# Two layers of a hybrid trunk on one core: reordered start, reordered down projections, key heads first

## The chip, the cores and the metric

The kernel runs on one core of one Trainium2 chip. The metric is the device time of one execution in microseconds, median of three runs; lower is better.

## The reference

The reference is a decoder trunk of two pre-norm residual layers over one sequence of 512 tokens with 1024 features, all in float32.

- Each layer adds `mixer(RMSNorm(x)) @ w_out` and then `(silu(h @ w_gate) * (h @ w_up)) @ w_down` with `h = RMSNorm(x)` and 2816 hidden features. A final RMSNorm follows.
- Layer 0 (even) mixes a gated 31-tap causal convolution with layer norm and differential attention (4 heads, rotary embedding).
- Layer 1 (odd) mixes a gated delta rule and forgetting attention, 4 heads of 128 each. For the delta rule, queries, keys and values go through a 4-tap causal convolution and SiLU. Queries and keys are then normalised by the root of their own sum of squares over the 128 features of a head, plus 1e-6. Two gates per head and token are computed from 12 extra columns of the input projection: `beta` (a sigmoid) and `g` (minus exp(a_log) times a softplus); forgetting attention has a third, `log_f`. `g` is summed cumulatively inside chunks, `log_f` over the whole sequence.

## The kernel before

**Layout.** Activations lie with features on partitions and tokens in the free dimension: `xT` and its scaled form `HH` are 8 chunks of 128 features by 512 tokens. Every weight and every activation that enters a large product is split into a high part (rounded to fp32r) and a low part (the rest), and a product is three matmuls: high by high, high by low, low by high (`product`, L1484). ScalarE makes the high part of a weight tile (`hi`), VectorE the low part (`lo`).

**Weight stream.** The weights come as 196 tiles of 128 by 1024 (512 KB) in the order in which they are used. SyncE's queue loads them through two raw buffers (the first tiles through two more, `first_raw`); the split copies lie in a ring of four, `wring`. A tile `t` is loaded once the low part of tile `t - 2` is done, and is split once TensorE has used tile `t - 4` (`tile_used`). Counted semaphores tie all of it together.

**Start (L485 to L506 SyncE, L669 on ScalarE, L1053 on VectorE, L1585 on TensorE).** The loads are `vec` (286 columns of per-channel constants, 143 KB), then chunks of x and weight tiles in turn. Three matmuls of 512 columns on zeros run first (`WARM`). Then come the value products of layer 0: four tiles of two chunks each, each chunk multiplied for 4 blocks of 128 tokens into banks 0 to 3 of PSUM, 96 matmuls. Only the first tile is handled in halves. The sum of squares for the norm is collected beside it (`ssq`), summed over features by eight small matmuls (`norm_stats`, at the entry "norm" of `even_order`, L131), and its reciprocal root (`rtok`) is spread over the partitions by `norm_spread`. All engines walk the same written order `even_order()`, each doing its own part of an entry: at ("v", a) ScalarE and VectorE split tile a + 4, at ("cw", c) VectorE builds filter weights.

**Feed-forward.** `gate_up` uses banks 0 to 3 of PSUM in turn, one per tile; VectorE multiplies each by the norm while copying it out (L993, counted by `evacuated`). The down product of layer 0 (`down`, L1728) holds its sums in all eight banks, one for each chunk of output features; that of layer 1 (`token_down`, L1998) also holds eight, two for each block of 128 tokens. Both wait, before their first matmul, for the last of the evacuations of gate and up. In the last four tiles of layer 1 the product goes bank by bank, and the first bank takes each of the four tiles as it arrives.

**Odd layer, first part (TensorE L1787 to L1831, ScalarE L783 to L831, VectorE L1276 to L1310).** Twelve tiles e = 0 to 11 give the convolution inputs: e = 0 to 3 queries, 4 to 7 keys, 8 to 11 values; a thirteenth tile (`HEAD_TILE`, with e = 3) gives the 12 gate columns. For each e, TensorE runs 24 matmuls. VectorE copies the result out (`cin`), splits a weight tile and runs taps 1 to 3 (L1289); ScalarE splits a weight tile, runs tap 0 (L799) and SiLU (L810). For queries and keys ScalarE then squares the result (L815), and TensorE sums the squares over the features by matmuls with one column (`token_sum`, 8 instructions for each e, since a float32 matmul is two). Keys and values are transposed on TensorE (`tok_transpose`, from e = 6 on) and copied back by ScalarE (`tok_copy`, L786). The gate values are computed in four steps on VectorE (`gates_1` to `gates_4`, at e = 5, 6, 7 and 9) with Exp and Ln on ScalarE in between. Their sums over time are matmuls with triangular and all-one matrices at e = 8: 4 instructions for `g`, 20 for `log_f`. `delta_scalars` (VectorE, e = 10) makes the scale factors; the transpose of `pairs` on TensorE (L1830, e = 11) waits for it. After that the delta rule, the attention and the remaining tiles run in an order written out as the string `PLAN`.

Of the kernel before, what the change touches and what calls it, by code (L numbers as in the profile page):

```python
# [19 lines left out]
P = 128  # L20
# [34 lines left out]
WARM = 3  # L55
# [75 lines left out]
def even_order():  # L131

    order = []
    order += [("v", 0), ("cw", 0), ("v", 1), ("cw", 1), ("v", 2), ("norm", 0), ("v", 3), ("norm_bc", 0), ("v_evac", 0), ("cw", 2)]
# [68 lines left out]
PLAN = ("ktttttkatbtatbtttttattattbtbttababttatabttabtatbabatbattabeeooaeotaeebooteeooaeeooeaoabteettootbeeab"  # L203
# [64 lines left out]
def build(nc, x_d, w_d, vec_d, row_d, const_d, rope_d, final_d, out_d):  # L268
# [54 lines left out]
    gtok, q = at("gtok", [NB, H], f32, q)  # L323
    lftok, q = at("lftok", [NB, H], f32, q)
    scal, q = at("scal", [6, NB, H], f32, q)
    total, cum, forget = scal[:, 0], scal[:, 1], scal[:, 2]
    kscal, qeps = (scal[:, 3], scal[:, 5]), scal[:, 4]
    gexp, q = at("gexp", [3, NB, H], f32, q)
    l2s, q = at("l2s", [NB, 8], f32, q)
# [47 lines left out]
    hrow, _ = at("hrow", [S], f32, at_z)  # L377
    rows, q = at("rows", [H, P], f32r, at_A + 3 * 2 * S * 4)
# [74 lines left out]
    x_loaded = [sem(f"x_loaded{n}") for n in range(5)]  # L453
    X_PART = (0, 1, 2, 2, 3, 3, 4, 4)
    first_loaded = [sem(f"first_loaded{n}") for n in range(FIRST - RAW)]
    gdn_mm, gdn_act, gdn_dve, gdn_pool = [[sem(f"gdn{n}_{e}") for n in range(2)] for e in ("products", "act", "dve", "pool")]
    const_loaded, vec_loaded, rope_loaded, small_loaded = map(sem, ("const_loaded", "vec_loaded", "rope_loaded", "small_loaded"))
# [31 lines left out]
    def _(sp):  # L489
# [4 lines left out]
        sp.dma_start(vec[:], vec_d).then_inc(vec_loaded, 16)  # L494
        load_x(0)
        sp.dma_start(raw[:, 0, 0:S], w_d[0][:, 0:S]).then_inc(sem("half_loaded"), 16)
        load_x(1)
        sp.dma_start(raw[:, 0, S:TILE], w_d[0][:, S:TILE]).then_inc(raw_loaded[0], 16)
        load_x(2)
        sp.dma_start(raw[:, 1], w_d[1]).then_inc(raw_loaded[1], 16)  # L500
        load_x(3)
        sp.dma_start(first_raw[:, 0], w_d[2]).then_inc(first_loaded[0], 16)
        load_x(4)
        sp.dma_start(first_raw[:, 1], w_d[3]).then_inc(first_loaded[1], 16)
        sp.dma_start(consts[:, 0:3].rearrange("p a b -> p (a b)"), const_d[:, 0:3 * P]).then_inc(const_loaded, 16)
        sp.dma_start(rowv[0:1, :], row_d).then_inc(small_loaded, 16)  # L506
# [92 lines left out]
    def _(act):  # L599
# [72 lines left out]
        for n in range(KD):  # L672
            act.wait_ge(x_loaded[X_PART[n]], 16)
            feed_hi_(0, n)
            if n < 2:
                act.wait_ge(raw_loaded[0] if n else sem("half_loaded"), 16)
                ins = nc.scalar.activation(wring[:, 0, 0, n * S:(n + 1) * S], raw[:, 0, n * S:(n + 1) * S], ACT.Copy)  # L677
                ins.then_inc(hi_ready[0] if n else sem("first_hi"), 1)
            elif n % 2 == 0:
                hi(n // 2)  # L680
            if n % 2:
                feed_square(0, n - 1)
                feed_square(0, n)
        def diff_exp(u):
# [98 lines left out]
        def tok_copy(m):  # L783

            act.wait_ge(sem("tok_t"), m + 1)
            nc.scalar.activation((ktok, vtok)[m // 4][:, :, m % 4], PS[:, TOK_BANK[m]].rearrange("p (b c) -> p b c", b=NB),  # L786
                                 ACT.Copy).then_inc(sem("tok_ready"), 1)

        for e in range(12):
            if e >= 7:  # L790
                tok_copy(e - 7)
# [10 lines left out]

            h = e % H
            act.wait_ge(sem("gconv_done"), e + 1)
            if e >= 10:
                act.wait_ge(sem("tok_t"), e - 5)
            if e in (8, 9):
                act.wait_ge(sem("l2_mm"), e - 1)
            dst = (qT[:, h], kT[:, h], sqb[:, e % 2])[e // 4]
            nc.scalar.activation(dst, hbuf[:, e % 2], ACT.Silu).then_inc(sem("gsilu"), 1)  # L810
            if e < 8:
                act.wait_ge(sem("gsilu"), e + 1)
                if e >= 2:
                    act.wait_ge(sem("l2_mm"), e - 1)
# [1280 lines left out]
```

## Time and profile before

| | us |
|---|---|
| median of 3 runs (1287.69 to 1289.47) | 1288.94 |
| the profiled execution | 1287.33 |
| its span, first to last instruction | 1285.5 |
| TensorE busy (6195 matmul instructions) | 1268.4 |
| VectorE busy | 671.3 |
| ScalarE busy | 493.6 |
| 16 DMA engines, mean rate | 91 GB/s |

An engine that is busy for nearly the whole span sets the time by the sum of its instructions; what it waits for is then read from the list of its waits, and what it does from a timeline of the stretch. A float32 matmul appears as two instructions, one of fp32r as one.

### The profile page before, as it was taken

The numbers are of one execution on the slowest core, as the hardware profiler recorded it, in microseconds if no ns is written. First come the engines' busy times: TensorE is split into PE (matmuls) and PEld (weight loads), VectorE is DVE, ScalarE is ACT, GpSimd is POOL, SyncE is SP. The second block draws the span as 40 slices with busy tenths as digits, with TensorE's granted clock in tenths as the row PEclk, the third lists the DMA queues.
The fourth block names the chain that finished last, engine by engine and source line by source line (L and its number), as shares of the span: only waits on it lengthen the run. The fifth ranks groups of instructions, "written<-read, shape, count | busy, mean of one in ns | idle before, by whom it ended". The sixth has DMA issues, their size and how long they took to land.

```text
span 1285.5 us, 16497 instructions
## 1 busy us (share of the span) xinstructions
PE 1268.4 (99%) x6195; PEld 1028.6 (80%) x6195; DVE 671.3 (52%) x967; ACT 493.6 (38%) x786; POOL 9.9 (1%) x17
## 2 busy tenths in 40 slices
PE   8999999999999999999999999999999999999998
PEld 6776648888888878888887988888888888887886
DVE  6677786544444442227757657545564444443224
ACT  6353455433333221115455244453433333322113
POOL 0000000000000000000000010000000000000000
PEclk9999999999999999999999999999999999999999
DMA  6232311322222222221221101011243443322221
GB/s 245 81 113 88 100 51 54 111 98 98 98 98 98 98 97 99 98 97 67 99 72 60 67 34 42 25 50 66 99 127 110 110 110 110 102 98 98 98 99 65
DMA packets 50434, 116.66 MB, mean 91 GB/s; under 512 B 21074, under 2 KB 21330, under 8 KB 50386
## 3 DMA queue, kind: packets, MB, share of 16 engines
q1 hardware_dynamic: 49474, 114.65, 26.8%
q10 hardware_dynamic: 912, 1.35, 0.4%
q8 instruction: 33, 0.54, 0.2%
q14 instruction: 15, 0.12, 0.0%
HBM read 107.43 MB, written 2.10 MB: 85 GB/s over the span
## 4 chain that ended last, share of the span: by engine, by line
PE 90%; DVE 4%; ACT 3%; issue 1%; DMA 1%; ACTq 0%; SPq 0%; DVEq 0%
PE PS L1480 89%; DMA raw<-w_stream 1%; DVE wring L1022 1%; ACT wring L608 1%; PE PS L1556 1%; DVE hbuf L1289 0%; DVE cacc L1166 0%; ACTq L731 0%; DVE resid L1455 0%; DVE outT L1471 0%; ACT HH L612 0%; ACT unread L921 0%; ACT L845 0%; DVE amax L1084 0%; ACT pbuf L690 0%
## 5 line engine op out<-in xcount | busy, mean ns | idle before, releaser
L1480 PE MATMUL PS<-HH,wring 128*128 128x512 f32 x3096 | 728.0, 393 | 0.0
L1480 PEld LDWEIGHTS PS<-HH,wring 128*128 128x128 f32 x3096 | 576.3, 188 | 118.7 <-issue 1.4
L1480 PE MATMUL PS<-AA,wring 128*128 128x512 f32 (+1 forms) x792 | 183.1, 390 | 1.1 <-DVE ubuf L993 0.8
L1480 PEld LDWEIGHTS PS<-AA,wring 128*128 128x128 f32 x792 | 148.2, 188 | 33.4 <-DVE ubuf L993 1.2
L993 DVE TENSOR_TENSOR ubuf<-PS,rstd 128x512 f32<-128x512 f32 x44 | 30.4, 690 | 191.2 <-PE PS L1480 191.2
L1015 DVE TENSOR_TENSOR wring<-raw,wring 128x1024 fp32r<-128x1024 f32 x36 | 44.1, 1226 | 149.6 <-ACT wring L664 149.6
L1480 PE MATMUL PS<-wring,AA 128*128 128x512 f32 x528 | 120.2, 389 | 1.3 <-DVE ubuf L993 0.8
L1480 PEld LDWEIGHTS PS<-wring,AA 128*128 128x128 f32 x528 | 98.9, 188 | 22.6 <-DVE ubuf L993 1.2
L1002 DVE TENSOR_TENSOR wring<-raw,wring 128x1024 fp32r<-128x1024 f32 x88 | 107.5, 1221 | 4.4 <-ACT wring L651 3.9
L608 ACT ACTIVATE wring<-raw 128x1024 fp32r<-128x1024 f32 x70 | 73.5, 1055 | 81.8 <-PE PS L1480 59.2
L1022 DVE TENSOR_TENSOR wring<-raw,wring 128x1024 fp32r<-128x1024 f32 x70 | 85.5, 1225 | 34.8 <-ACT wring L608 34.7
L646 ACT ACTIVATE AA<-ubuf 128x512 f32 x44 | 27.8, 633 | 191.8 <-DVE ubuf L1000 191.8
L664 ACT ACTIVATE wring<-raw 128x1024 fp32r<-128x1024 f32 x36 | 38.2, 1061 | 155.5 <-PE PS L1480 155.5
L651 ACT ACTIVATE wring<-raw 128x1024 fp32r<-128x1024 f32 x88 | 92.0, 1045 | 3.9 <-DMA raw<-w_stream 3.9
L640 ACT ACTIVATE gbuf<-gbuf 128x512 f32<-128x512 f32 x44 | 27.8, 632 | 116.9 <-DVE gbuf L993 116.9
L993 DVE TENSOR_TENSOR gbuf<-PS,rstd 128x512 f32<-128x512 f32 x44 | 30.4, 690 | 37.4 <-PE PS L1480 37.1
L1480 PE MATMUL PS<-wring,HH 128*128 128x512 f32 x192 | 46.6, 395 | 1.6 <-issue 0.9
L1480 PEld LDWEIGHTS PS<-wring,HH 128*128 128x128 f32 x192 | 35.3, 188 | 9.8 <-ACT wring L677 1.5
L690 ACT ACTIVATE pbuf<-PS,amax 128x128 f32<-128x128 f32 (+3 forms) x32 | 16.6, 523 | 46.4 <-DVE amax L1084 46.3
L1000 DVE TENSOR_TENSOR ubuf<-gbuf,ubuf 128x512 f32<-128x512 f32 x44 | 30.4, 692 | 5.8
L612 ACT ACTIVATE HH<-xT,vec 128x512 fp32r<-128x512 f32 x32 | 22.9, 716 | 21.7 <-DVE xT L983 18.5
L945 DVE SCALAR_TENSOR_TENSOR HH<-xT,vec,HH 128x512 fp32r<-128x512 f32 x32 | 24.0, 750 | 12.1 <-ACT HH L612 11.3
(272 smaller groups left out, 1046.3 us busy)
## 6 DMA issues: line engine op xcount, KB each, us to landing
raw<-w_stream SPq DMA_DIRECT2D x194, 512.0 KB, 3.2
reps<-ub SPq DMA_DIRECT2D x32, 66.5 KB, 2.1
resid<-turned SPq DMA_DIRECT2D x16, 128.0 KB, 4.7
xT<-x_t SPq DMA_DIRECT2D x3, 512.0 KB, 8.0
out_t<-outT SPq DMA_DIRECT2D x3, 512.0 KB, 2.6
reps_b<-ub SPq DMA_DIRECT2D x16, 66.5 KB, 2.1
reps<-ub ACTq DMA_DIRECT2D x16, 66.5 KB, 2.4
first_raw<-w_stream SPq DMA_DIRECT2D x2, 512.0 KB, 9.3
```

Of the source, the lines that this page charges most:

```text
L608: nc.scalar.activation(wring[:, t % RING, 0], raw_tile(t), ACT.Copy).then_inc(hi_ready[t % RING], 1)
L640: nc.scalar.activation(gbuf[:, c], gbuf[:, c], ACT.Silu).then_inc(sem("gate_silu"), 1)
L646: nc.scalar.activation(AA[:, bass.ds(r * 2 + c, 1), 0].rearrange("p a b -> p (a b)"), ubuf[:, c], ACT.Copy).then_inc(sem("ffn_hi"), 1)
L651: nc.scalar.activation(wring[:, t % RING, 0], raw[:, t % RAW], ACT.Copy).then_inc(hi_ready[t % RING], 1)
L664: nc.scalar.activation(wring[:, t % RING, 0], raw[:, t % RAW], ACT.Copy).then_inc(hi_ready[t % RING], 1)
L945: V.scalar_tensor_tensor(HH[:, n, 1], xT[:, n], vcol(V_NORM + KD * s + n), HH[:, n, 0].bitcast(f32), ALU.mult, ALU.subtract).then_inc(h_re ...
L993: V.tensor_tensor(buf[:, c], PS[:, 2 * c + u], rstd[:], ALU.mult).then_inc(evacuated, 1)
L1000: V.tensor_tensor(ubuf[:, c], gbuf[:, c], ubuf[:, c], ALU.mult).then_inc(sem("ffn_mul"), 1)
L1002: V.tensor_tensor(wring[:, t % RING, 1], raw[:, t % RAW], wring[:, t % RING, 0].bitcast(f32), ALU.subtract).then_inc(lo_ready[t % RING], 1)
L1015: V.tensor_tensor(wring[:, t % RING, 1], raw[:, t % RAW], wring[:, t % RING, 0].bitcast(f32), ALU.subtract).then_inc(lo_ready[t % RING], 1)
L1022: V.tensor_tensor(wring[:, t % RING, 1], raw_tile(t), wring[:, t % RING, 0].bitcast(f32), ALU.subtract).then_inc(lo_ready[t % RING], 1)
L1480: return nc.tensor.matmul(out, lhsT, rhs, start=start, stop=stop)
```

## The change

It has four parts.

- **Start.** `vec` is loaded in two pieces: its first 8 columns behind the first chunk of x, the rest behind the constants. The first two weight tiles (`HALVED = 2`) are loaded and split in halves, and x comes in six parts. The value products of a chunk wait by parts: high by high for all four token blocks, then high weight by low x, then low weight by high x (`value_chunk`). The matmuls on zeros are two of 512 and two of 128 columns. In `even_order` the entry ("norm", 0) comes before ("v", 2) and ("cw", 1) after it; TensorE still runs `norm_stats` behind the third value tile.
- **Down products.** Both begin with banks 4 to 7 and wait for the evacuations only before the first bank of 0 to 3. In layer 1, the last four tiles are taken by both banks of token block 0 as they arrive.
- **Keys first.** The weight tiles of the keys come first (e = 0 to 3), queries are e = 4 to 7. Keys are transposed at e = 2 to 5. Their sums of squares come from ScalarE, four squarings of 128 by 128 with an accumulated sum for each head in `tok_copy`, and no longer from matmuls; `token_sum` stays for the queries, at e = 6 to 9.
- **Gates.** The steps sit at e = 4, 5, 6 and 8. `g` and `log_f` are summed by the same two matmuls of 32 columns (4 instructions), and VectorE adds the totals of earlier blocks with three small additions. `delta_scalars` moves to e = 9, the root of the key sums to e = 8. `PLAN` begins with "tk" in place of "kt".

```diff
-WARM = 3
+HALVED = 2
+WARM = (S, S, P, P)
...
-    order += [("v", 0), ("cw", 0), ("v", 1), ("cw", 1), ("v", 2), ("norm", 0), ("v", 3), ...
+    order += [("v", 0), ("cw", 0), ("v", 1), ("norm", 0), ("v", 2), ("cw", 1), ("v", 3), ...
...
-        sp.dma_start(vec[:], vec_d).then_inc(vec_loaded, 16)
         load_x(0)
+        sp.dma_start(vec[:, 0:KD], vec_d[:, 0:KD]).then_inc(vec_loaded, 16)
+        for t in range(HALVED):
+            sp.dma_start(raw[:, t, 0:S], w_d[t][:, 0:S]).then_inc(half_loaded[t], 16)
+            load_x(2 * t + 1)
+            sp.dma_start(raw[:, t, S:TILE], w_d[t][:, S:TILE]).then_inc(raw_loaded[t], 16)
+            load_x(2 * t + 2)
...
+            pe.wait_ge(feed_hi, k + 1)
+            pe.wait_ge(half_hi[t] if split else hi_ready[t], 1)
+            for b in range(NB):
+                mm(PS[:, b], HH[:, k, 0, blk(b)], whi, k == 0, False)
+            pe.wait_ge(h_ready, k + 1)
+            for b in range(NB):
+                mm(PS[:, b], HH[:, k, 1, blk(b)], whi, False, False)
+            pe.wait_ge(half_lo[t] if split else lo_ready[t], 1)
+            for b in range(NB):
+                last = mm(PS[:, b], HH[:, k, 0, blk(b)], wlo, False, k == KD - 1)
...
         def down(s, td):
-            pe.wait_ge(evacuated, E_GU0 + 2 * KF)
+            pe.wait_ge(norm_rstd, 2)
...
-                for n in range(KD):
+                for n in list(range(RING, KD)) + list(range(RING)):
+                    if k == 0 and n == 0:
+                        pe.wait_ge(evacuated, E_GU0 + 2 * KF)
...
         def tok_copy(m):
             act.wait_ge(sem("tok_t"), m + 1)
+            if m < H:
+                for b in range(NB):
+                    ins = nc.scalar.activation(key_sq[:, b], PS[:, TOK_BANK[m], blk(b)], ACT.Square, accum_out=l2s[:, b, m:m + 1])
+                ins.then_inc(sem("key_sums"), 1)
...
-            if 2 <= e < 10:
-                c = e - 2
+            if 6 <= e < 10:
+                c = e - 6
...
-                g_all = gtok[:].rearrange("p a b -> p (a b)")
-                mm(PS[:, 6, 0:16], ones, g_all)
-                mm(PS[:, 6, 16:32], cums, g_all)
-                for b in range(NB):
-                    for j in range(b + 1):
-                        last = mm(PS[:, 6, 32 + 4 * b:36 + 4 * b], cums if j == b else ones, lftok[:, j], j == 0, j == b)
+                both = glf[:].rearrange("p a b c -> p (a b c)")
+                mm(PS[:, 6, 0:32], ones, both)
+                last = mm(PS[:, 6, 32:64], cums, both)
...
-            if e >= 6:
+            if 2 <= e < 6:
+                tok_transpose(e - 2)
+            elif e >= 10:
                 tok_transpose(e - 6)
```

## Rows read from the trace of the kernel before

**Rows 1.** The page, busy microseconds, share of span, instructions of each engine:
```profile
PE 1268.4 (99%) x6195; PEld 1028.6 (80%) x6195; DVE 671.3 (52%) x967; ACT 493.6 (38%) x786; POOL 9.9 (1%) x17
```

**Rows 2.** Waits of TensorE: who, released by whom, total us, times, longest:
```profile
PE PS L1480 <- DVE ubuf L993: 1.6, 2, 0.8
PE PS L1830 <- DVE pairs L1267: 1.5, 1, 1.5
PE PS L1480 <- DVE rtok L966: 0.8, 1, 0.8
PE PS L1480 <- ACT sqb L815: 0.7, 1, 0.7
```

**Rows 3.** Timeline of the start: start, us, engine, line, instruction, idle before it:
```profile
4.25 0.72 ACT L612 ACTIVATE HH<-xT,vec 128x512 fp32r<-128x512 f32 x1 [1.99 <-DMA xT<-x_t]
5.11 0.63 ACT L677 ACTIVATE wring<-raw 128x512 fp32r<-128x512 f32 x1
...
6.57 5.74 PE L1480 MATMUL PS<-wring,HH 128*128 128x512 f32 x24 [0.70 <-DVE wring L1059]
...
7.84 0.63 ACT L677 ACTIVATE wring<-raw 128x512 fp32r<-128x512 f32 x1
...
13.17 11.16 PE L1480 MATMUL PS<-wring,HH 128*128 128x512 f32 x48 [0.87 <-issue]
...
21.37 1.48 DVE L959 TENSOR_TENSOR ssq<-ssq,squares 128x512 f32<-128x512 f32 x2
...
24.98 5.75 PE L1480 MATMUL PS<-wring,HH 128*128 128x512 f32 x24
...
28.59 1.06 ACT L608 ACTIVATE wring<-raw 128x1024 fp32r<-128x1024 f32 x1 [6.79 <-DMA raw<-w_stream]
```

**Rows 4.** Windows of the start: busy us of each engine, TensorE clock, DMA share, GB/s:
```profile
0.00:6.50 6.50, 4.54 (x6) 1.69 (x6) 1.35 (x2) 2.86 (x4) 0.92 (x9) 1.00 0.65 181
6.50:13.00 6.50, 5.74 (x24) 4.38 (x24) 3.98 (x6) 5.33 (x9) 0.00 (x0) 1.00 0.99 398
```

**Rows 5.** Timeline of TensorE and VectorE in the odd layer's first part:
```profile
608.63 0.69 DVE L1280 TENSOR_TENSOR cin<-PS,rstd 128x512 f32<-128x512 f32 x1
...
659.43 0.95 PE L1480 MATMUL PS<-consts,sqb 128*128 128x1 f32 x8
660.23 0.61 PE L1480 MATMUL PS<-gtok,consts 128*128 128x16 f32 x4
660.69 2.38 PE L1480 MATMUL PS<-lftok,consts 128*128 128x4 f32 x20
662.92 0.64 PE L1775 MATMUL PS<-consts,kT 128*128 128x128 f32 x4
663.31 7.31 PE L1480 MATMUL PS<-HH,wring 128*128 128x512 f32 x24
...
671.66 5.72 PE L1480 MATMUL PS<-HH,wring 128*128 128x512 f32 x24
...
685.25 0.33 PE L1830 MATMUL PS<-consts,pairs 128*128 128x128 f32 x1 [1.51 <-DVE pairs L1267]
```

**Rows 6.** Windows in the odd layer's first part, columns as in Rows 4:
```profile
662.00:663.00 1.00, 1.00 (x11) 1.00 (x11) 0.47 (x1) 1.00 (x2) 0.00 (x0) 1.00 0.00 0
...
664.00:665.00 1.00, 1.00 (x4) 0.71 (x4) 0.96 (x2) 0.00 (x0) 0.00 (x0) 0.50 0.14 20
```

**Rows 7.** Groups of ScalarE by shape: count, busy us, mean ns, idle before:
```profile
L608 ACT ACTIVATE wring<-raw 128x1024 fp32r<-128x1024 f32 x70 | 73.5, 1055 | 81.8 <-PE PS L1480 59.2 <-DMA raw<-w_stream 22.6
...
L863 ACT ACTIVATE G<-PS 128x128 f32<-128x128 f32 x16 | 4.2, 278 | 6.8 <-PE PS L1480 6.8
...
L815 ACT ACTIVATE sqb<-kT 128x512 f32<-128x512 f32 x4 | 2.5, 631 | 0.1
```

**Rows 8.** Groups of VectorE from 600 to 700 us, columns as in Rows 7:
```profile
L1289 DVE SCALAR_TENSOR_TENSOR hbuf<-cin,vec,hbuf 128x512 f32<-128x512 f32 x36 | 27.0, 750 | 0.8
```

**Rows 9.** Timeline near the end of the last down product:
```profile
1259.76 19.97 PE L1480 MATMUL PS<-wring,AA 128*128 128x512 f32 x87 [0.52 <-DVE wring L1022]
```

More of the change, by code:

```diff
@@ L133, in even_order @@
     order = []
-    order += [("v", 0), ("cw", 0), ("v", 1), ("cw", 1), ("v", 2), ("norm", 0), ("v", 3), ("norm_bc", 0), ("v_evac", 0), ("cw", 2)]
+    order += [("v", 0), ("cw", 0), ("v", 1), ("norm", 0), ("v", 2), ("cw", 1), ("v", 3), ("norm_bc", 0), ("v_evac", 0), ("cw", 2)]
     order += [("qk", (0, part)) for part in range(4)] + [("qk_evac", 0), ("cw", 3)]
@@ L674, in _ @@
             feed_hi_(0, n)
[L675 to L678, printed above, removed]
+            if n < 2 * HALVED:
+                t, half = n // 2, slice(n % 2 * S, (n % 2 + 1) * S)
+                act.wait_ge((half_loaded, raw_loaded)[n % 2][t], 16)
+                nc.scalar.activation(wring[:, t, 0, half], raw[:, t, half], ACT.Copy).then_inc((half_hi, hi_ready)[n % 2][t], 1)
             elif n % 2 == 0:
@@ L801, in _ @@
                 tok_copy(5)
[L803 to L814, printed above, removed]
-                nc.scalar.activation(sqb[:, e % 2], dst, ACT.Square).then_inc(sem("gsq"), 1)
             if e == 5:
@@ L1583, in tile_part, with value_chunk @@
                 last.then_inc(tile_used, 1)
+        def value_chunk(k):
+            t = T_IN0 + k // 2
+            whi, wlo = wpair(t % RING, slice(k % 2 * S, (k % 2 + 1) * S))
+            split = k < 2 * HALVED and k % 2 == 0
+            pe.wait_ge(feed_hi, k + 1)
[8 more added lines that the diff above has]
+                last = mm(PS[:, b], HH[:, k, 0, blk(b)], wlo, False, k == KD - 1)
+            return last
         pe.wait_ge(sem("warm_zero"), 1)
-        for n in range(WARM):
-            mm(PS[:, 6], rstd[:, 0:P], rstd[:]).then_inc(sem("warm_mm"), 1)
+        for n in WARM:
+            mm(PS[:, 6, 0:n], rstd[:, 0:P], rstd[:, 0:n])
         for kind, a in even_order():
             if kind == "v":
-                if a == 0:
-                    pe.wait_ge(sem("first_hi"), 1)
-                    pe.wait_ge(sem("first_lo"), 1)
-                else:
-                    arrived(T_IN0 + a)
-                for k in (2 * a, 2 * a + 1):
-                    if k == 1:
-                        arrived(T_IN0)
-                    w = wpair((T_IN0 + a) % RING, slice(k % 2 * S, (k % 2 + 1) * S))
-                    pe.wait_ge(h_ready, k + 1)
-                    for b in range(NB):
-                        last = product(PS[:, b], (HH[:, k, 0, blk(b)], HH[:, k, 1, blk(b)]), w, k == 0, k == KD - 1)
+                last = value_chunk(2 * a)
+                last = value_chunk(2 * a + 1)
                 last.then_inc(tile_used, 1)
-            elif kind == "norm":
-                pe.wait_ge(const_loaded, 16)
-                norm_stats(0, 7)
+                if a == 2:
+                    pe.wait_ge(const_loaded, 16)
+                    norm_stats(0, 7)
             elif kind == "norm_bc":
@@ L1764, in tok_transpose @@
         def tok_transpose(m):
-            pe.wait_ge(sem("gsilu"), m + 5)
+            pe.wait_ge(sem("gsilu"), m + 1 if m < H else m + 5)
             if m == 6:
@@ L2006, in _ @@
             pe.wait_ge(sem("ffn_lo"), KF + k + 1)
-            for n in range(NB):
+            for n in (2, 3, 0, 1):
+                if k == 0 and n == 0:
+                    pe.wait_ge(evacuated, E_GU1 + 2 * KF)
                 for u in range(2):
```

129 lines of the change are left out of this document (78 added, 51 removed).

## The prediction, as recorded before the changed kernel was run

> **What bounds the kernel now.** I read the table of engines first. TensorE is busy 1268.4 us of a span of 1285.5; the other engines have 600 us or more to spare [rows 1]. So only two things can move the time: TensorE's own instructions, and the 17.1 us in which it has none. The second view is the list of TensorE's waits [rows 2]; the reader is to see that it is short and that nearly every row names one place. The third is the timeline of the two stretches in which these places lie, the start [rows 3] and the first part of the odd layer [rows 5]. The profiled execution took 1287.33 us, 1.6 below the median of 1288.94; I sum against the profile and carry the difference over.
>
> One rate is used throughout: 24 large matmuls take 5.56 us. The row at 13.17 gives 11.16 / 48 = 0.2325 us each, the row at 671.66 gives 5.72 with the last one's tail [rows 3, 5]; call it 0.232.
>
> **Start.** Before, the first value product starts at 6.57, when VectorE's low half is done. By parts it needs only ScalarE's half, 5.11 + 0.63 = 5.74 [rows 3]. In addition, 139 KB of `vec` no longer lie ahead of the first weights: at 398 GB/s that is 0.36 us, at 181 GB/s 0.79 [rows 4]. I take 0.4, so 5.35; the upper end is 5.75 (no help from the order), the lower 5.0. The second chunk needs the half whose split starts at 7.84, ready at 8.47 before and about 8.05 now, and TensorE comes to it at 5.35 + 12 x 0.232 = 8.13: just in time. The second tile, for which it waited 0.87 (13.17), now arrives in halves. It comes due at 5.35 + 5.56 = 10.9; its first half is about 650 KB less far back in the queue than the whole tile was, and needs 0.63 of splitting instead of 1.06, so I expect no wait. From there the 96 products and the eight sums (0.8, rows 5 at 659.43 to 660.23) end at 5.35 + 96 x 0.232 + 0.8 = 28.4. The sums need `ssq`, which ends at 22.85 before; the same chain on ScalarE and VectorE moves up by 0.4 to 0.8 as its inputs do, and TensorE asks at 5.35 + 72 x 0.232 = 22.05: 0 to 0.4 of new wait.
>
> Before, the products ended at 24.98 + 5.75 = 30.73 and the spread of the norm waited 0.76 more, until 31.49, for `rtok` [rows 2, 3]. That came from ScalarE's order: its root stood behind a weight split that waited for its load until 28.59. Now the root stands ahead of that split, and is ready some 3 us before it is needed. What else moves past it: VectorE's filter weights for group 1 and one low part run later; TensorE needs that tile only two tiles on, so it is covered. Gain at the start: 31.49 - 28.4 = 3.1, less 0.1 for tight spots, **3.0** (bounds 1.8 and 3.5). The new small load (32 bytes a partition) is the same instruction count on SyncE for the first chunk, and two more issues before the fourth tile; the queue was ahead of the engines there.
>
> **Down products.** Both waits on the last evacuation are 0.8 each, together 1.6 [rows 2]. The first four banks give 12 matmuls, 2.8 us of cover, and the weights and the first activations were ready long before. Gain **1.55** (bounds 1.0 and 1.6). In the last tiles of layer 1, TensorE had 9 matmuls (2.1 us) while the last tile was being split, and waited 0.52 [rows 9]; with 18 matmuls the wait goes: **0.5**. The first bank's signal comes 2 us later, but the end is set by the last bank, so that costs nothing.
>
> **Odd layer, first part.**
> - Key sums on TensorE: four groups of 8 instructions. A group takes 660.23 - 659.43 = 0.80 [rows 5]: 3.2 us removed, and all of it on the path, as TensorE never pauses there. Its replacement on ScalarE is four squarings with a sum for each key head. The nearest row is the same form in the delta rule, 278 ns each [rows 7], so 1.1 us, less the 0.63 squaring that is dropped [rows 7].
> - Gate sums: 24 instructions from 660.23 to 662.92, 2.7 us, become 4; the 4 of `g` took 660.69 - 660.23 = 0.46 [rows 5]. **2.2**. The three additions that replace them are small VectorE work beside 5.6 us of matmuls.
> - Waits: the 0.7 for the first squares (`sqb`) falls to about 0.1, since the transpose that now stands there needs SiLU only, 0.63 earlier [rows 2, 7]. The 1.5 for `pairs` goes: `delta_scalars` comes one tile (5.6 us) earlier. **2.1** together.
> - Clock: at 664 the granted clock is 0.50, that is 1.2 GHz instead of 2.4, right after some 36 tiny instructions between 659.43 and 663.31; before that, at 662, it is 1.00 [rows 5, 6]. The tile that runs then takes 7.31 us instead of 5.72, 1.6 more [rows 5]. After the change the longest run of tiny ones is 12 (8 sums and 4 for the gates), a third of it. So I take **1.6** back (bounds 0 and 1.6).
>
> What could be late next is the relay of ScalarE and VectorE. Where keys are copied, one turn is: copy and squares 1.6, split on ScalarE 1.0, split on VectorE 1.2, three taps 2.3 (3 x 0.75), SiLU 0.63, square for a query 0.63 [rows 7, 8]: 7.4 us, against 5.6 to 6.4 of TensorE. Four turns are of this kind, e = 3 to 6, and the relay loses about 1.2 us in each. It begins with a reserve, as at e = 3 TensorE has a second tile (5.6 us); I carry it forward turn by turn and find it 4.5 us behind at e = 7, and about 1 at e = 11, since later turns lack the copy and the square: 1.0 + 1.2 + 2.3 + 0.63 = 5.1, and up to 5.7 where the gate steps fall in them. Each use of its results on TensorE is one or two tiles later, so no wait until the last transpose, about 0.2; and the delta rule's first product of VectorE comes some 0.3 later than now, relative to TensorE. Minus **0.5** (bounds 0 and 2.5). Stage: 3.2 + 2.2 + 2.1 + 1.6 - 0.5 = **8.6**, bounds 4.8 and 9.2.
>
> **Sum:** 3.0 + 1.55 + 0.5 + 8.6 = 13.65 us. The profiled execution would fall to 1273.7, the median to 1288.94 - 13.65 = 1275.3.
>
> **A rule and the trace.** Before 664 TensorE is busy in every window, with 11 instructions a microsecond, and the clock falls all the same [rows 6]. The Trainium skill, page "TensorE: Matmul & The Clock Gate", section "Part 1: The HAM clock gate (the "warmup" mystery)", ties the lower clock to an idle TensorE and the higher one to sustained activity. Taken by the word, the drop here was not caused by the tiny matmuls, and removing them would not bring the clock back; the sum would be 12.05 and the median 1276.9. [...]
>
> **Rivals.**
> - A: the half-clock stretch stays, or appears elsewhere, for instance behind the 12 tiny ones or at the start, where fewer columns run on zeros. For it: one fall in 1285 us is one sample of a cause I only infer. Against it: the longest run of tiny instructions shrinks to a third. 1276.9. Chance 0.17.
> - B: the start stays bound by its loads: the smaller pieces land no sooner, TensorE catches up with each chunk and waits there. For it: DMA moved only 181 GB/s in the first 6.5 us. Against it: at the 398 GB/s after 6.5 us [rows 4] a weight tile and its two chunks of x, 1 MB, take 2.6 us, and TensorE needs 5.56 for them. Gain 0.5 instead of 3.0: 1277.8. Chance 0.10.
> - C, the other side: the relay of ScalarE and VectorE takes over the pace of the stage. The stage now lasts from the first copy at 608.6 to the `pairs` at 685.3, 76.7 us [rows 5]; after the change 12 turns of TensorE would last about 68. If turns took 7.4 us throughout, they would last 89, 12 us more than now; with the 5 us gained elsewhere taken off, the total would be 1296. The point from which it decides is a mean turn of (76.7 + 5.05) / 12 = 6.8 us, where those gains are used up. Against it: only four turns carry the key copies, and the reserve covers them. Chance 0.06, half of it at a partial price (1278 to 1284), half slower.
> - D: the down products do not start earlier, because the wait for the evacuation hid one for a weight tile: 1276.9. Chance 0.02.
>
> **The numbers.** The forecast, 1275.3, has 0.65. A measurement of this kernel can tell about 0.2% (2.6 us) from no change. Range 1272.5 to 1279.0: the lower end takes every upper bound of the gains (14.9) and the spread of the runs, the upper end covers A and B, singly or together. Faster by over 0.2%: 0.95; within: 0.02; slower: 0.03, from C.
>
> **What would show it.** Right: the first large matmul at 5.2 to 5.8, no wait at the second tile, and `norm_spread` at 28.2 to 29; no row of TensorE waiting for `ubuf` L993 or for `pairs`; the granted clock at 1.00 in the whole odd layer; 32 fewer instructions of `sqb` sums and 20 fewer for `log_f`. Wrong: a wait of TensorE for ScalarE or VectorE between e = 3 and e = 11 of over 1 us, or a new half-clock row.

## The result, and the profile after

| | before | after |
|---|---|---|
| median | 1288.32 us (1285.88 to 1289.47, 4 runs) | 1273.68 us (1273.32 to 1274.18, 4 runs) |
| the profiled execution | 1287.33 | 1273.32 |
| its span | 1285.5 | 1271.5 |
| TensorE busy, instructions | 1268.4, 6195 | 1259.8, 6145 |

The ratio is 0.9889 [0.9877, 0.9901]: 14.6 us less. Between the two profiled executions it is 14.0. The forecast was 1275.3.

The page after, busy time and instructions of each engine, answers to [rows 1]:

```profile
PE 1259.8 (99%) x6145; PEld 1022.6 (80%) x6145; DVE 671.5 (53%) x971; ACT 496.5 (39%) x816; POOL 9.9 (1%) x17
```

TensorE has 50 instructions (32 key sums and 20 gate sums less, 2 on zeros more) and 8.6 us of busy time less; the other 5.4 us were time without work. The waits of TensorE after, columns as in [rows 2]:

```profile
PE PS L1499 <- POOL rstd L573: 1.3, 1, 1.3
PE PS L1898 <- DVE G L1379: 0.8, 1, 0.8
PE PS L1499 <- ACT WT L706: 0.8, 1, 0.8
...
PE PS L1499 <- ACT wring L682: 0.3, 1, 0.3
```

None of the four rows of [rows 2] is left. What stands there now also stood in the list before, at places that the change does not touch; only the last row shown is new: the first product now waits for ScalarE's half of the weights, 0.3 us, where it waited 0.70 for VectorE's [rows 3].

The start after, columns as in [rows 3]:

```profile
3.90 0.72 ACT L616 ACTIVATE HH<-xT,vec 128x512 fp32r<-128x512 f32 x1 [1.63 <-DMA vec<-vectors]
...
5.44 0.63 ACT L682 ACTIVATE wring<-raw 128x512 fp32r<-128x512 f32 x1 [0.83 <-DMA raw<-w_stream]
...
6.22 16.67 PE L1499 MATMUL PS<-wring,HH 128*128 128x512 f32 x72 [0.27 <-ACT wring L682]
...
25.92 0.18 DVE L979 RECIPROCAL rtok<-nst 128x4 f32<-128x4 f32 x1 [0.27 <-ACT nst L634]
...
29.12 1.05 PE L1499 MATMUL PS<-consts,rtok 128*128 128x128 f32 x8
```

The 72 products now stand in one row: there is no wait at the second tile. `rtok` is ready at 26.1, three microseconds before the spread at 29.12 reads it. That spread began at 31.49 before.

TensorE in the odd layer's first part, answers to [rows 5]:

```profile
652.58 0.95 PE L1499 MATMUL PS<-consts,sqb 128*128 128x1 f32 x8
653.39 0.61 PE L1499 MATMUL PS<-glf,consts 128*128 128x32 f32 x4
653.83 5.73 PE L1499 MATMUL PS<-HH,wring 128*128 128x512 f32 x24
...
672.14 0.27 PE L1857 MATMUL PS<-consts,pairs 128*128 128x128 f32 x1
...
678.56 0.71 PE L1499 MATMUL PS<-rows,pick 128*128 128x512 f32 x2
```

The tile behind the tiny instructions takes 5.73 us where it took 7.31, and `pairs` has no wait. The window over it, columns as in [rows 4], has the granted clock at 1.00 (third column from the right):

```profile
650.00:660.00 10.00, 10.00 (x56) 8.55 (x54) 7.40 (x10) 7.01 (x10) 0.00 (x0) 1.00 0.25 80
```

Milestones of both traces show where the 14.0 us came from. The shift is the start of the same instruction before, minus after.

| milestone | before | after | shift | gained in the stretch | forecast |
|---|---|---|---|---|---|
| spread of the norm | 31.49 | 29.12 | 2.37 | 2.37 | 3.0 |
| product of e = 2 in the odd layer | 607.63 | 604.12 | 3.51 | 1.14 | half of 1.55 |
| `rows,pick` behind the last transpose | 691.67 | 678.56 | 13.11 | 9.60 | 8.6 |
| down product of layer 1 | 1158.98 | 1144.92 | 14.06 | 0.95 | half of 1.55 |
| end of TensorE | 1279.73 | 1264.77 | 14.96 | 0.90 | 0.5 |
| end of the span | 1285.5 | 1271.5 | 14.0 | -0.96 | 0 |

The last line is the odd one: TensorE ends 15.0 us earlier and the kernel only 14.0. These are TensorE and VectorE at the end of the changed kernel:

```profile
1235.82 28.95 PE L1499 MATMUL PS<-wring,AA 128*128 128x512 f32 x127
...
1247.90 0.69 DVE L1474 TENSOR_TENSOR resid<-resid,PS 128x512 f32<-128x512 f32 x1 [2.48 <-PE PS L1499]
...
1249.38 0.15 DVE L1478 TENSOR_SCALAR nst<-ost 128x1 f32<-128x1 f32 x1 [0.79 <-ACT unread L934]
1249.45 0.68 DVE L1474 TENSOR_TENSOR resid<-resid,PS 128x512 f32<-128x512 f32 x1
...
1265.92 0.68 DVE L1474 TENSOR_TENSOR resid<-resid,PS 128x512 f32<-128x512 f32 x1
```

And the same sums of token block 0 before:

```profile
1260.83 0.69 DVE L1455 TENSOR_TENSOR resid<-resid,PS 128x512 f32<-128x512 f32 x1 [1.22 <-PE PS L1480]
...
1263.45 0.69 DVE L1455 TENSOR_TENSOR resid<-resid,PS 128x512 f32<-128x512 f32 x1 [0.99 <-PE PS L1480]
```

Each token block passes through a relay: sum on VectorE, square on ScalarE (`unread`), a small step on VectorE (`nst`), second sum, its square, root, output. From the second sum of block 0 to the end of the span it is 22.05 us in both kernels (1285.5 - 1263.45 and 1271.5 - 1249.45). So this relay, not TensorE's last bank, sets the end. Before, the second sum waited only for its bank (0.99 idle, released by TensorE). After, both banks of block 0 are done at 1247.9, but the second sum stands in VectorE's order behind `nst`, and `nst` waits 0.79 for ScalarE's square. That puts it at 1249.45, 1.5 us behind its bank. The very last sum starts at 1265.92, 1.15 us after TensorE has ended; before, it was 0.2 us (1279.94 and 1279.73).

### The profile page after: what moved, and what is told of

Read it like the earlier page. It is cut to its first block, busy times and chain, and to the rows that moved or that the text cites. A ratio compares the mean times of both kernels' runs of the same rounds, so it can differ in the third digit from the quotient of the medians.

```text
span 1271.5 us, 16433 instructions
## 1 busy us (share of the span) xinstructions
PE 1259.8 (99%) x6145; PEld 1022.6 (80%) x6145; DVE 671.5 (53%) x971; ACT 496.5 (39%) x816; POOL 9.9 (1%) x17
## 4 chain that ended last, share of the span: by engine, by line
PE 93%; DVE 3%; ACT 2%; issue 1%; ACTq 0%; DMA 0%; SPq 0%; DVEq 0%
PE PS L1499 92%; PE PS L1575 1%; DVE cacc L1180 0%; ACTq L737 0%; DVE resid L1474 0%; DVE outT L1490 0%; ACT unread L934 0%; DMA raw<-w_stream 0%; PE PS L1803 0%; DVE wring L1035 0%; ACT L858 0%; DVE amax L1098 0%; DVE hbuf L1306 0%; ACT pbuf L696 0%; ACT wring L612 0%
## 5 line engine op out<-in xcount | busy, mean ns | idle before, releaser
L1019 DVE TENSOR_TENSOR AA<-ubuf,AA 128x512 f32 x44 | 30.1, 685 | 0.0
```

The source lines that it names most:

```text
L1019: V.tensor_tensor(AA[:, bass.ds(r * 2 + c, 1), 1].rearrange("p a b -> p (a b)"), ubuf[:, c], AA[:, bass.ds(r * 2 + c, 1), 0].rearrange("p ...
```

## The experiments

All kernels are the changed one with the edit shown, except `before_gates_6`, which is the kernel before with an edit. Each was timed in five rounds beside the kernel before. The changed kernel gave 1273.68 at first and 1273.61 (1273.49 to 1273.9) as `after_same` on another chip, so differences from 1273.6 of half a microsecond can be read across chips.

### The tail: the old bank order, and the relay freed

`tail_old` puts the last four tiles of layer 1 back:

```diff
-        for k in range(KF - RING, KF - 1):
-            arrived(T_DN1 + k)
-            for u in range(2):
-                token_down(0, u, k)
...
+        for n in range(NB):
+            for u in range(2):
+                for k in range(KF - RING, KF):
+                    if n + u == 0:
+                        arrived(T_DN1 + k)
+                    last = token_down(n, u, k)
+                last.then_inc(sem("token_down"), 1)
```

> The changed kernel with the old order of the last four tiles of the last down product (token block 0's first bank takes each tile as it arrives, then its second bank). Theory T: the end is set by the relay of VectorE and ScalarE, which starts when token block 0's second sum is taken and then runs 22.05 us whatever TensorE does; the new order delivers the first bank 2 us later, so both sums come together. Then this kernel has the 0.5 us wait of TensorE for the last tile again and yet is not slower: 0 to 0.8 us faster than the changed kernel (1272.9 to 1273.7), with the second sum taken about 14.5 us earlier than in the kernel before. Theory P, my prediction's step: the last bank of TensorE sets the end, so this is 0.5 us slower (1274.2).

Measured: 1273.38 us (1273.2 to 1275.19), ratio 0.9891 [0.9874, 0.9907]. No difference from the changed kernel. Its trace is of the longest execution, 1275.19 us, whose start was longer (see the clock at the start); TensorE and the two sums of block 0:

```profile
1247.62 19.97 PE L1499 MATMUL PS<-wring,AA 128*128 128x512 f32 x87 [0.52 <-DVE wring L1035]
1248.69 0.69 DVE L1474 TENSOR_TENSOR resid<-resid,PS 128x512 f32<-128x512 f32 x1 [1.22 <-PE PS L1499]
...
1251.31 0.69 DVE L1474 TENSOR_TENSOR resid<-resid,PS 128x512 f32<-128x512 f32 x1 [0.99 <-PE PS L1499]
```

The wait of 0.52 for the last tile [rows 9] is back and costs nothing: the second sum again follows its bank, and from it to the end of the span (1273.4) it is 22.1 us, as before.

`tail_relay` keeps the new bank order and moves `nst` behind the second sum, for all blocks but the last:

```diff
-            dve.wait_ge(sem("final_sq"), 2 * n + 1)
-            V.tensor_scalar(nst[:, n:n + 1], ost[:, 0, 2 * n:2 * n + 1], 1.0 / D, 1e-6, ALU.mult, ALU.add).then_inc(sem("final_ms"), 1)
+            if n == NB - 1:
+                dve.wait_ge(sem("final_sq"), 2 * n + 1)
+                V.tensor_scalar(nst[:, n:n + 1], ost[:, 0, 2 * n:2 * n + 1], 1.0 / D, 1e-6, ALU.mult, ALU.add).then_inc(sem("final_ms"), 1)
...
             final_sum(1)
+            if n < NB - 1:
+                dve.wait_ge(sem("final_sq"), 2 * n + 1)
+                V.tensor_scalar(nst[:, n:n + 1], ost[:, 0, 2 * n:2 * n + 1], 1.0 / D, 1e-6, ALU.mult, ALU.add).then_inc(sem("final_ms"), 1)
```

> The changed kernel with one step of the tail moved on VectorE: for token blocks 0 to 2 the small scale-and-add of the first half's sum of squares stands behind the second residual addition instead of ahead of it. Theory T (the relay sets the end): the relay's turn falls from 4.87 us to about 4.0, TensorE's last bank sets the end again, and the time falls by 0.8 to 1.1 us (1272.7). Theory P (TensorE's last bank sets the end already): no change, 1273.7.

Measured: 1272.46 us (1271.96 to 1272.64), ratio 0.9885 [0.9868, 0.9901]; 1.2 below the changed kernel, with no overlap of the runs. VectorE in its trace:

```profile
1247.60 1.29 DVE L1474 TENSOR_TENSOR resid<-resid,PS 128x512 f32<-128x512 f32 x2 [2.48 <-PE PS L1503]
1249.07 0.15 DVE L1485 TENSOR_SCALAR nst<-ost 128x1 f32<-128x1 f32 x1 [0.19 <-ACT unread L934]
```

Both sums now run back to back, and the span ends 5.7 us after TensorE (1264.46 to 1270.1) in place of 6.7. In token block 2 the second sum waits for TensorE again, 1.43 us at 1259.06, so here TensorE's banks set the end. That settles the tail: theory T, the relay, holds, and the microsecond that the new bank order gives TensorE reaches the end only with this second edit.

### The start: bytes ahead, and the order of the norm

`vec_whole` loads `vec` in one piece again, at the place of its first piece:

```diff
-        sp.dma_start(vec[:, 0:KD], vec_d[:, 0:KD]).then_inc(vec_loaded, 16)
+        sp.dma_start(vec[:], vec_d).then_inc(vec_loaded, 16)
```

> The changed kernel with the whole of the constants (143 KB, 1144 bytes a partition) loaded in second place instead of their first 8 columns (32 bytes a partition) there and the rest behind. Theory S (a load of 32-byte pieces is dear): the first product of ScalarE, which waited for the small load until 3.90 us, starts no later, and the first matmul stays at 6.2 or comes earlier; time 1273.4 to 1273.8. Theory B (bytes ahead decide, as predicted): the loads behind it land 0.35 to 0.8 us later, the first matmul starts at 6.6 to 7.0 and the time rises by 0.4 to 0.8 us, to 1274.3.

Measured: 1275.23 us (1273.65 to 1275.97), ratio 0.9905 [0.9888, 0.9922]. TensorE at its start:

```profile
6.36 3.10 PE L1495 MATMUL PS<-wring,HH 128*128 128x512 f32 x12 [0.41 <-ACT wring L681]
10.35 13.85 PE L1495 MATMUL PS<-wring,HH 128*128 128x512 f32 x60 [0.89 <-ACT wring L681]
...
30.43 1.05 PE L1495 MATMUL PS<-consts,rtok 128*128 128x128 f32 x8
```

The first product is only 0.14 late: the first half of the first weights lands 3.9 us after its issue, against 3.8. The second half lands 7.0 us after its issue against 5.6, TensorE waits 0.89 for it, and the spread comes at 30.43 in place of 29.12. So in this execution the 139 KB cost 1.3 us, not the 0.4 that I took, and not at the load where I had looked for it. Theory B holds in part. The price is not a fixed one: the four times spread over 2.3 us, the lowest equals the changed kernel's, and what the others have beyond 1274.67, the time of the trace, is not shown.

`norm_late` puts back the old place of the norm:

```diff
-    order += [("v", 0), ("cw", 0), ("v", 1), ("norm", 0), ("v", 2), ("cw", 1), ("v", 3), ...
+    order += [("v", 0), ("cw", 0), ("v", 1), ("cw", 1), ("v", 2), ("norm", 0), ("v", 3), ...
```

> The changed kernel with the old order of the entries (filter weights 1, value tile 2, norm), all else as changed. Theory: TensorE's wait of 0.76 us for the reciprocal root comes from ScalarE's root standing behind a weight split that waits for its load; it returns in full, time 1274.4. Rival: by starting earlier TensorE gave the split more time, so that the order alone brought nothing: 1273.7.

Measured: 1275.41 us (1273.52 to 1275.42), ratio 0.9902 [0.9886, 0.9919]. Its start:

```profile
6.75 18.22 PE L1499 MATMUL PS<-wring,HH 128*128 128x512 f32 x72 [0.79 <-ACT wring L682]
...
30.09 0.18 DVE L979 RECIPROCAL rtok<-nst 128x4 f32<-128x4 f32 x1 [0.27 <-ACT nst L634]
...
31.20 1.05 PE L1499 MATMUL PS<-consts,rtok 128*128 128x128 f32 x8
```

This run does not settle what it was made for. `rtok` is ready at 30.27, 4.2 us later than in the changed kernel and 1.2 us after the moment (29.12) at which that one reads it. But in this execution the 72 products took 18.22 us in place of 16.67, so TensorE came to the spread late on its own account and no wait stands there. By that subtraction the order would cost 1.2 us; no wait row shows it, and one of the four executions took 1273.52 us, no more than the changed kernel. What the order alone is worth in the changed kernel, between nothing and 1.2 us, stays open. The 18.22 is a second matter; the next section takes it up.

### The clock at the start

The profiled executions of `norm_late` and of `tail_old` (18.30 us for the 72 products) had this longer start. By their times two more of `norm_late` had it (1275.42 both, the profiled one 1275.41), and none of the four of `after_same`. Before the first product TensorE runs the matmuls on zeros. Their weight loads in the changed kernel show the level of the clock:

```profile
2.33 0.34 PEld L1499 LDWEIGHTS PS<-rstd 128*128 128x128 f32 x1 [0.52 <-issue]
...
4.04 0.34 PEld L1499 LDWEIGHTS PS<-rstd 128*128 128x128 f32 x1 [0.52 <-issue]
```

The same instruction takes 0.19 us later on, so here the engine is at the lower of its two levels, 1.2 GHz. The window 6.6 to 8.2 us has 8 matmuls in the changed kernel, but 4 in the execution of `tail_old` with 18.30: there the rise to 2.4 GHz came after the first products. The granted-clock column says 1.00 in both windows, so at the very start it cannot be used; counts and durations can.

`warm_short` takes half of the columns on zeros away:

```diff
-WARM = (S, S, P, P)
+WARM = (S, P)
```

> The changed kernel with one matmul of 512 and one of 128 columns on zeros instead of two and two: TensorE is then idle from about 3.5 us until the first product at 6.2. Theory W: the clock rises later in all executions, the first 72 products take 18.3 us instead of 16.7 or more, and the median is 1275.3 or up to 1.6 above that. Rival: how long TensorE works on zeros does not matter, the clock rises by itself: 1273.7.

Measured: 1275.3 us (1275.09 to 1276.04), ratio 0.99 [0.9882, 0.9918]; `after_same`, of the same set, 1273.61. Its first products:

```profile
6.16 19.44 PE L1499 MATMUL PS<-wring,HH 128*128 128x512 f32 x72 [2.33 <-ACT wring L682]
```

The first product is as early as ever, behind 2.33 us without work, the 72 take 2.8 us longer, and the median is 1.7 up. The lowest of its times, 1275.09, lies above the highest of `after_same`, 1273.9, so all four seem to have it: theory W holds. `relay_warm` goes the other way, with `tail_relay`'s edit and a third short matmul on zeros:

```diff
-WARM = (S, S, P, P)
+WARM = (S, S, P, P, P)
```

> The changed kernel with the tail's small scale-and-add behind the second residual addition (the step tried alone before) and one more matmul of 128 columns on zeros, which fills TensorE until about 6.2 us. Theory T: 1.0 us off the tail. Theory W: no execution with a late rise of the clock. Together 1272.2 to 1272.8 in all executions. Rival to W: late rises as often as without it, executions at 1274.3.

Measured: 1272.53 us (1272.26 to 1273.08), ratio 0.988 [0.9863, 0.9898]: the 1.1 of the relay and nothing else. Four executions without a late rise prove little, since `after_same` had none either; whether the third short matmul helps stays open.

### The gate sums

`gates_24` sums `log_f` by the old 20 instructions of 4 columns, behind the four new ones, and drops the three additions:

```diff
-                last = mm(PS[:, 6, 32:64], cums, both)
+                mm(PS[:, 6, 32:64], cums, both)
+                for b in range(NB):
+                    for j in range(b + 1):
+                        last = mm(PS[:, 6, 48 + 4 * b:52 + 4 * b], cums if j == b else ones, lftok[:, j], j == 0, j == b)
```

> The changed kernel with the old 20 instructions for the sums of log_f put back behind the 4 new ones (and VectorE's three small additions left out), so that 32 instructions with 1 to 32 columns follow each other at e = 8. Theory C (few columns for long enough lower the clock): 2.2 us for the instructions, and a half-clock stretch right behind them that costs 1.6 us, in most executions: 1275.9 to 1277.5, profile with a half-clock row near 658 us. Rival I (the fall at 664 us in the kernel before had nothing to do with them; it needs an idle TensorE): 2.2 us and no half-clock row: 1275.9, with no execution above 1276.5.

Measured: 1279.08 us, ratio 0.9921 [0.9906, 0.9936], in two groups: 1275.52 and 1275.57 with a mean clock of 0.999, and 1279.08, 1279.1 and 1279.26 with 0.996. The profiled execution is of the first group:

```profile
653.33 2.82 PE L1496 MATMUL PS<-glf,consts 128*128 128x32 f32 x24
656.01 5.75 PE L1496 MATMUL PS<-HH,wring 128*128 128x512 f32 x24
```

656.01 - 653.33 = 2.68 in place of 0.44: 2.2 us for the instructions. In three of five executions 3.5 us came on top, with the lower mean clock. None of these was profiled, so where in them the clock was low is not shown. The clock's share is thus an event that happens in an execution or does not.

`before_gates_6` puts 2 instructions of 16 columns in place of the 20, in the kernel before. It leaves out the totals of earlier blocks, so the sums of `log_f` start anew in each block of 128 tokens:

```diff
-                for b in range(NB):
-                    for j in range(b + 1):
-                        last = mm(PS[:, 6, 32 + 4 * b:36 + 4 * b], cums if j == b else ones, lftok[:, j], j == 0, j == b)
+                last = mm(PS[:, 6, 32:48], cums, lftok[:].rearrange("p a b -> p (a b)"))
```

> The kernel before with the 20 instructions for log_f replaced by 2 (the totals of earlier blocks are left out of log_f's sum, so the forgetting attention of later blocks is computed with another decay), nothing else changed: 18 tiny instructions fewer, 2.0 us. Theory C: the half-clock stretch at 664 us goes as well and the profile shows the granted clock at 1.00 in the odd layer: 3.6 us less than the kernel before in the executions that have the stretch, and the spread of its times narrows. Rival I: 2.0 us less and the stretch stays.

Measured: 1283.81 us (1283.31 to 1284.76) against 1288.02 of the kernel before, ratio 0.9966 [0.9954, 0.9978]: 4.2 us. TensorE at the same place:

```profile
660.71 0.37 PE L1480 MATMUL PS<-lftok,consts 128*128 128x16 f32 x2
660.94 0.63 PE L1775 MATMUL PS<-consts,kT 128*128 128x128 f32 x4
661.33 5.73 PE L1480 MATMUL PS<-HH,wring 128*128 128x512 f32 x24
```

The sums of `log_f` take 0.23 us in place of 2.23, which is 2.0. The tile behind them takes 5.73 in place of 7.31 [rows 5], 1.6 more. The key sums are still on TensorE here (8 instructions at 659.45), so the 20 decided over this stretch. The other 0.6 of the 4.2 probably lies in executions that have more such stretches, of which no trace was kept: the runs of the kernel before spread over 3.3 us (mean clocks 0.996 to 0.999), those of this one over 1.5 (0.998 to 0.999).

### The relay in the odd layer

`squares_x3` runs each of ScalarE's four squarings three times, the extra ones into scratch:

```diff
+                for b in range(NB):
+                    nc.scalar.activation(key_sq2[:, b], PS[:, TOK_BANK[m], blk(b)], ACT.Square, accum_out=ost[:, 0, b:b + 1])
+                for b in range(NB):
+                    nc.scalar.activation(key_sq3[:, b], PS[:, TOK_BANK[m], blk(b)], ACT.Square, accum_out=ost[:, 1, b:b + 1])
                 for b in range(NB):
                     ins = nc.scalar.activation(key_sq[:, b], PS[:, TOK_BANK[m], blk(b)], ACT.Square, accum_out=l2s[:, b, m:m + 1])
```

> The changed kernel with the four accumulated squarings of each key head done three times on ScalarE (8 more, about 2.0 us in each of the turns e = 3 to 6; the two extra results go to scratch). It measures how much reserve the relay of ScalarE and VectorE has. Theory R (prediction's step: a reserve of a turn at e = 3, used to within about 1 us at e = 11, and recovered at 0.5 to 1.2 us a turn from e = 7 on): of the 8 us added about 3 to 4 are recovered and 1 is reserve, so TensorE waits 3 to 4.5 us for SiLU between e = 9 and the last transpose: 1277 to 1278. Rival: the relay is far from TensorE's pace, nothing shows: 1273.7.

Measured: 1280.97 us (1280.71 to 1281.1), ratio 0.9941 [0.9928, 0.9955], 7.3 above the changed kernel. Its largest wait of TensorE, then TensorE's timeline, then the window over the first of the two stretches:

```profile
PE PS L1505 <- ACT sqb L848: 3.6, 2, 2.5
```

```profile
649.26 1.05 PE L1505 MATMUL PS<-consts,sqb 128*128 128x1 f32 x8 [2.52 <-ACT sqb L848]
650.17 7.33 PE L1505 MATMUL PS<-HH,wring 128*128 128x512 f32 x24
658.62 1.05 PE L1505 MATMUL PS<-consts,sqb 128*128 128x1 f32 x8 [1.12 <-ACT sqb L848]
...
659.98 7.32 PE L1505 MATMUL PS<-HH,wring 128*128 128x512 f32 x24
```

```profile
650.00:660.00 10.00, 8.88 (x40) 7.09 (x39) 4.89 (x9) 9.85 (x28) 0.00 (x0) 0.83 0.14 52
```

Each of the four key heads gets 8 more squarings of 0.25 us, 8 us in all. Of these TensorE waits 3.6, at e = 7 and 8, where it needs the squares of the queries; later turns are shorter and there is no wait at the last transpose. Each wait is followed by a tile at 1.2 GHz, 7.33 us in place of 5.75: 1.6 us each, and the window has a granted clock of 0.83. 3.6 + 3.2 = 6.8 of the 7.3.

The reserve of the relay can be read from the changed kernel itself, from ScalarE's squares of the queries e = 5 and 6:

```profile
641.92 0.63 ACT L842 ACTIVATE sqb<-qT 128x512 f32<-128x512 f32 x1
...
649.21 0.63 ACT L842 ACTIVATE sqb<-qT 128x512 f32<-128x512 f32 x1
```

They end at 642.55 and 649.84, and TensorE sums them at 646.18 and 652.58: 3.6 and 2.7 us to spare. The sums at e = 7 come when 6 of the 8 us have been added: 6 - 3.6 = 2.4, and the wait is 2.52. Those at e = 8 come after all 8: 8 - 2.7 = 5.3, and TensorE is by then late by 2.52 + 1.6 + 1.12 = 5.2. So the reserve here is 2.7 us, and beyond it both waits cost more than their length, as a slow tile followed each.

### The down products

`down_old` puts both waits and both bank orders back:

```diff
-            pe.wait_ge(norm_rstd, 2)
+            pe.wait_ge(evacuated, E_GU0 + 2 * KF)
...
-                for n in list(range(RING, KD)) + list(range(RING)):
+                for n in range(KD):
```

> The changed kernel with the old bank order and the old wait for the last evacuation at the start of both down products. Theory: both waits of 0.8 us for the evacuation return: 1273.7 + 1.55 = 1275.2, the profile with two rows of TensorE waiting for ubuf. Rival: in the changed kernel something else released by the same time hides one of them: 1274.5.

Measured: 1275.7 us (1275.46 to 1277.96), ratio 0.9907 [0.9892, 0.9922]; 2.0 above the changed kernel. Its wait and one of the two places; then the same place in the changed kernel:

```profile
PE PS L1499 <- DVE ubuf L1006: 1.8, 2, 0.9
```

```profile
472.68 7.50 PE L1499 MATMUL PS<-AA,wring 128*128 128x512 f32 x32 [0.88 <-DVE ubuf L1006]
```

```profile
471.80 4.47 PE L1499 MATMUL PS<-AA,wring 128*128 128x512 f32 x19
```

472.68 - 0.88 = 471.80: the new order removes the whole wait and brings none. A wait costs more than its row, though. `down_old` is 0.12 us ahead of the changed kernel at the spread of the norm (29.00 against 29.12) and 0.97 behind at the product of e = 2 (605.09 against 604.12): 1.1 us for a wait of 0.88. Of the rest, 0.16 is the tail of the last matmul before the wait (its record lasts 0.39, where the next one otherwise starts 0.23 after it), and 0.08 a wider spacing of the first two matmuls behind it.

### The best version

The small load of `vec` waits its turn on SyncE, whose issues stand 0.46 us apart, and it lies between the first chunk of x and the first weights. `relay_warm_vec` is `relay_warm` with that load issued by ScalarE:

```diff
-        sp.dma_start(vec[:, 0:KD], vec_d[:, 0:KD]).then_inc(vec_loaded, 16)
+        nc.scalar.dma_start(vec[:, 0:KD], vec_d[:, 0:KD]).then_inc(vec_loaded, 16)
         act.wait_ge(sem("warm_zero"), 1)
```

> As the kernel with the tail step and one more matmul on zeros, and the first 8 columns of the constants are loaded from ScalarE's queue, so that the first chunk of x and the first weights are issued on SyncE at 0.74 and 1.19 us and each later load 0.46 us earlier. Theory B (the loads pace the first product): the first product starts at 5.8 to 6.0 instead of 6.2, a gain of 0.2 to 0.45 us: 1272.1. Rival (the queues are bound by the rate of the first microseconds, not by the time of issue, or the matmuls on zeros now bind): no change against the kernel beside it.

Measured: 1271.83 us (1271.66 to 1272.2), ratio 0.9874 [0.9857, 0.9892]. Its start:

```profile
4.55 0.61 ACT L682 ACTIVATE wring<-raw 128x512 fp32r<-128x512 f32 x1
...
5.84 16.59 PE L1503 MATMUL PS<-wring,HH 128*128 128x512 f32 x72
...
28.66 1.05 PE L1503 MATMUL PS<-consts,rtok 128*128 128x128 f32 x8
```

The first half is split at 4.55 and the spread comes at 28.66, in place of 5.65 and 29.25 in `relay_warm`. The half is ready at 5.16, but the first product starts at 5.84, right behind the matmuls on zeros and without a wait: now these bind, and no longer the load. It is 1.8 us below `after_same` in the same set, and beats both kernels of the case.

## Why the prediction was right, step by step

The median fell to 1273.68, within the range and 1.6 below the forecast; the sum, 13.65, stands against 14.0 of the profiled execution. That it fits this well is in part luck: by the milestones its parts were off by -0.6 (start), +0.5 (down products), -0.6 (last tiles) and +1.0 (odd stage), and these cancel. The bounds of the stage follow from its terms as 5.0 and 9.1, not 4.8 and 9.2; nothing hangs on that.

- **Start, 3.0 forecast, 2.37 measured.** The step that failed is "so 5.35". The first product came at 6.22 and the spread at 29.12, both later than the signs I had given. I had let the first weights land 0.4 earlier for the 139 KB taken away ahead of them. But their first half was split at 5.44, later than before (5.11) [rows 3]. Its load is issued at 1.65 us in both kernels, third behind a load of x and one of `vec`; it lands 3.8 us later, against 3.4 before and 3.9 in `vec_whole`. So the bytes brought this load nothing; they showed at the second half. Why it landed no earlier stays open in part: in ten traces with this start it takes 3.5 to 4.3 us. `relay_warm_vec`, with the small load on another queue, issues it at 1.19 and has it after 3.2 us. The expected absence of a wait at the second tile held, and `rtok` went off the path as forecast, 3.0 us ahead.
- **Down products, 1.55 forecast, 2.1 measured.** The two waits of 0.78 went, as forecast, and `down_old` brought them back: 2.0 in the median, 1.8 in its wait row. The term was too small because it took a wait for the length of its row; by `down_old` a wait here costs 1.1.
- **Last tiles, 0.5 forecast, -0.06 measured.** The wait [rows 9] went, as forecast; the sentence that failed is that "the end is set by the last bank". It is set by VectorE and ScalarE, who start when the second sum of block 0 can. `tail_old` and `tail_relay` showed it from both sides.
- **Key sums, gate sums and waits of the odd stage, 3.2, 2.2 and 2.1.** The 32 and 20 instructions are gone, `gates_24` gave 2.2 back, and neither `sqb` nor `pairs` has a wait. The 3.2 of the key sums was read from the trace and has no run of its own.
- **The relay in the odd stage, -0.5 forecast.** It cost nothing that a row shows. The squarings stand 0.25 us apart (0.272 each in the mean, where [rows 7] had 0.278), and the four turns with key copies took 7.3 us in the mean, as forecast, but the last SiLU is over about 1 us before the transpose needs it. The stage gained 9.60; 3.2 + 2.2 + 2.2 for both waits + 1.6 are 9.2. The other 0.4 is about what two waits cost beyond their rows in `down_old`, but no run shows it here. Rival C did not come; `squares_x3` shows its mechanism to be real, beyond a reserve of 2.7 us at e = 8; at the last transpose it is the 1 us just named, as forecast.
- **Clock, 1.6 forecast.** The tile runs at 2.4 GHz again. Here the forecast weighed a rule against the trace, and the runs decide for the trace: `before_gates_6` took 18 tiny instructions away, TensorE was as busy as before around them, and the tile went from 7.31 to 5.73 us. The Trainium skill, page "TensorE: Matmul & The Clock Gate", section "Part 1: The HAM clock gate (the "warmup" mystery)", ties the lower clock to an idle TensorE. That is not the whole of it in this kernel, but the rule is not wrong either: in `squares_x3` both low stretches follow a wait of TensorE, of 2.52 and of 1.12 us. A wait alone did not always bring it: behind the 1.51 us for `pairs` in the kernel before, the tile took 5.71 us. Rival A did not come in the odd layer. At the start it came in single executions of experiments, which is the place I had named, and `warm_short` brought it in all four, by their times, at 1.7 us.
- **The spread of the runs.** The forecast took a half-clock stretch as a fixed cost of the kernel before. It is an event that an execution has or not, of 1.6 us where it was traced. The kernel before spread over 3.6 us in the first set, the changed one over 0.9; that is probably also why the medians differ by 14.6 and the profiled executions by 14.0.

## What to carry to other kernels

Before a wait of the busiest engine is removed near the end, follow the engines behind it to the last instruction: if their own chain has a constant length from some point, only that point's time matters, and a small step in their order can hold it back. At a start that loads bound, look for the cost of what lies ahead in the queue at each load behind it: 139 KB did not move the first one and cost 1.3 us at a later one, and a small load on a queue of its own let the first one land earlier. A removed wait of the busiest engine can give more than its row. Many matmuls of a few columns can cost more than their own time: 20 of them took 2.2 us, and in some executions the clock took 1.6 us or more on top, which shows as spread between runs and not in every profile.

## What was not expected of the hardware

- In the kernel before, the clock fell behind tiny matmuls without any idle time of TensorE ahead of it [rows 5, 6]. It depends on the execution: with `gates_24`, 3 of 5 were 3.5 us longer at a lower mean clock, though none of the three was traced.
- A wait of 1.12 us, with tiny matmuls behind it, was followed by a tile of 7.32 us, at 1.2 GHz (`squares_x3`).
- A wait of 0.88 us in its row cost 1.1 us of the time (`down_old`).
- The granted-clock column reads 1.00 in the first microseconds while weight loads take 0.34 us in place of 0.19.
- Squarings of 128 by 128 with an accumulated sum follow each other on ScalarE every 0.25 us, though each is shown with a read of the accumulator of 0.2 beside it. First and last of four, from the timeline of ScalarE in the changed kernel:

```profile
627.74 0.26 ACT L794 ACTIVATE key_sq<-PS 128x128 f32<-128x128 f32 x1
...
628.49 0.29 ACT L794 ACTIVATE key_sq<-PS 128x128 f32<-128x128 f32 x1
```
